# The first block's attention with queries on partitions in the values product, and the softmax division moved to its eviction

## What is computed

```python
o_mla  = rms_norm(mla_attention(h_mla, ...), mla_out_norm[l])       # 6 heads, q.k over 96, v 64 wide
o_diff = diff_attention(h_diff, ..., diff_norm[l], ...)             # 6 heads, two score maps of 32, v 64 wide
o_ch   = rms_norm(chunk_attention(h_ch, chunk_rel_bias[l]), chunk_out_norm[l])   # 4 heads of 64
x = x + jnp.concatenate([o_mla, o_diff, o_ch], axis=-1) @ w_out[l]
x = x + conv_ffn(rms_norm(x, ffn_norm[l]), ...)
```

## Time and profile before

| | us |
|---|---|
| median of 3 runs (lowest, highest) | 3262.74 (3247.85, 3288.86) |
| the profiled execution's own time | 3253.76 |
| its span, first to last instruction | 3252.1 |
| PE busy | 3127.5 (96%) |
| POOL busy | 1364.6 (42%) |
| DVE busy | 1323.3 (41%) |
| ACT busy | 839.6 (26%) |
| mean granted TensorE clock | 0.972 |

### The profile page before, as it was taken

How to read it: one execution, slowest core, us unless ns; L and a number is a source line. 1 busy time by engine, 2 the same in 40 slices (tenths; PEclk the granted TensorE clock), 3 DMA queues, 4 the chain that set the end, 5 groups by cost and what they waited for, 6 DMA issues and landing times.

```text
span 3252.1 us, 40121 instructions
## 1 busy us (share of the span) xinstructions
PE 3127.5 (96%) x14094; PEld 2430.5 (75%) x14094; DVE 1323.3 (41%) x2699; ACT 839.6 (26%) x1855; POOL 1364.6 (42%) x924
## 2 busy tenths in 40 slices
PE   7999999999989999989999999999999999999998
PEld 6666788888656788878666678888686667788886
DVE  5574434243664434353741641121437417411113
ACT  2346211121454212121333320011213333210112
POOL 5210555554211555555223445555452234455552
PEclk9989999999989999999999999999999999999999
DMA  7310566665311566655223546666452235466663
GB/s 251 104 52 27 175 194 193 193 209 180 98 40 53 184 194 194 192 183 175 91 86 115 157 154 187 195 201 193 149 175 91 85 117 159 154 189 190 204 193 101
DMA packets 136516, 494.05 MB, mean 152 GB/s; under 512 B 15280, under 2 KB 15536, under 8 KB 136112
## 3 DMA queue, kind: packets, MB, share of 16 engines
q0 software_dynamic: 66240, 241.20, 24.3%
q1 hardware_dynamic: 68544, 245.40, 23.7%
q10 hardware_dynamic: 1584, 5.40, 0.5%
HBM read 489.84 MB, written 2.10 MB: 151 GB/s over the span
## 4 chain that ended last, share of the span: by engine, by line
PE 93%; DVE 3%; ACT 1%; issue 1%; DMA 0%; POOL 0%; SPq 0%; DVEq 0%; POOLq 0%; ACTq 0%
PE ps L482 25%; PE ps L483 24%; PE ps L484 24%; PE ps L635 6%; PE ps L658 5%; PE ps L648 2%; PE ps L591 1%; PE ps L593 1%; PE ps L592 1%; PE ps L831 1%; PE ps L545 1%; PE ps L859 0%; PE ps L850 0%; DMA w_raw<-weights 0%; DVE lo L962 0%
## 5 line engine op out<-in xcount | busy, mean ns | idle before, releaser
L482 PE MATMUL ps<-hi,w_hi 128*128 128x512 f32 x3216 | 1286.9, 400 | 37.5 <-POOL w_lo L455 15.5
L483 PE MATMUL ps<-hi,w_lo 128*128 128x512 f32 x3216 | 1262.5, 393 | 0.0
L484 PE MATMUL ps<-lo,w_hi 128*128 128x512 f32 x3216 | 1261.4, 392 | 0.0
L455 POOL TENSOR_TENSOR w_lo<-w_raw,w_hi 128x1024 fp32r<-128x1024 f32 x460 | 1106.9, 2406 | 94.2 <-DMA w_hi<-weights 84.9
L450 POOL DMA_DIRECT2D w_hi<-weights x460 | 261.4, 568 | 1751.0 <-PE ps L484 1613.5
L482 PEld LDWEIGHTS ps<-hi,w_hi 128*128 128x128 f32 x3216 | 609.3, 189 | 228.8 <-issue 85.9
L484 PEld LDWEIGHTS ps<-lo,w_hi 128*128 128x128 f32 x3216 | 609.3, 189 | 130.4
L483 PEld LDWEIGHTS ps<-hi,w_lo 128*128 128x128 f32 x3216 | 609.9, 190 | 119.8
L1008 DVE CUSTOM_DVE_ANT_0 pr<-ps,kc 128x128 f32<-128x128 f32 (+1 forms) x208 | 88.8, 427 | 375.7 <-PE ps L635 375.7
L1499 ACT ACTIVATE pT<-ps 128x128 f32<-128x128 f32 (+1 forms) x248 | 97.8, 394 | 372.2 <-PE ps L648 371.9
L1647 ACT ACTIVATE ps<-hb,col 128x512 f32<-128x512 f32 x88 | 68.6, 782 | 381.1 <-DVE hb L991 381.1
(11 more groups left out here) (282 smaller groups left out, 3090.1 us busy)
## 6 DMA issues: line engine op xcount, KB each, us to landing
w_raw<-weights SPq DMA_DIRECT2D x460, 512.0 KB, 3.6
w_hi<-weights POOLq DMA_DIRECT2D x460, 512.0 KB, 4.0
x<-xt SPq DMA_DIRECT2D x8, 256.0 KB, 10.5
out<-x SPq DMA_DIRECT2D x8, 256.0 KB, 2.0
kc<-k ACTq DMA_DIRECT2D x1, 1281.0 KB, 5.6
bias<-relb ACTq DMA_DIRECT2D x2, 512.0 KB, 5.4
bias<-relb ACTq DMA_DIRECT2D x1, 1024.0 KB, 4.8
praw<-pt ACTq DMA_DIRECT2D x2, 512.0 KB, 3.6
```

Of the source, the lines that this page charges most:

```text
L455: nc.gpsimd.tensor_tensor(wlo[s][:, :], raw[s][:, :], whi[s][:, :].bitcast(F32), ALU.subtract).then_inc(w_split, 1)
L482: nc.tensor.matmul(out_ap, w[0], xx[0], start=first, stop=False)
L483: nc.tensor.matmul(out_ap, w[1], xx[0], start=False, stop=False)
L484: return nc.tensor.matmul(out_ap, w[0], xx[1], start=False, stop=last)
```

## The change

- The values product swaps its operands: the transposed weights (128 x 128) are stationary, the values (64 columns) are streamed, and the output has 128 queries on the partitions and 64 channels wide. It goes into the bank that its transposes had, a ring of 3.
- `p` is no longer divided for all keys. DVE evicts each task's 64 columns with the division (`tensor_scalar` by 1/sum) and squares and sums them by a second instruction. For diff heads one small factor, lambda times sum 1 over sum 2, is applied to the second map.
- The output norms' factors come from these sums: no squares on ACT, no sum or spread matmuls (L736, L746, L761, and the last L554 and L545 before `w_out`). The rows are scaled on DVE, and 8 tiles are transposed at the end (`turn_chunk`, 4 transposes each) into banks from which ACT and DVE take the high and low half.
- The slopes go into the queries, so the six `slope_times_distance` tables go away.
- The tasks are in the order diff 0 to 7, chunk 0 to 7, diff 8 to 23, MLA, chunk 8 to 15. Of the dense units only `dq0` and `dk0` remain ahead of the values; 12 units are spread over turns 0 to 23, and the MLA queries, keys and values take turns 24 to 36.
- `tables()` is split: distances first, before the input norm; `angles` is in DVE's side of turn 2, `signed_sine` in that of turn 5.

```diff
+ORDER_1 = ["cq0", "ck0", "cc0", "cc1", "cc2", "dq1", "stats", "dk1", "kr", "sp0", "sp1", "dq2", "dk2", "cq1", "ck1",
+           "Q0", "K0", "Q1", "V0", "V1", "Q2", "Q3", "K1", "Q4", "Q5", "K2", "V2", "V3"]
+FULL = ["cq0", "ck0", "cc0", "cc1", "cc2", "dq1", "dk1", "kr", "dq2", "dk2", "cq1", "ck1"]
+ITEM_AT = {24: "Q0", 25: "K0", 26: "Q1", 27: "V0", 28: "V1", 29: "Q2", 30: "Q3", 31: "K1", 32: "Q4", 33: "Q5", 34: "K2",
+           35: "V2", 36: "V3"}
+TILES_1 = 4 + len(ORDER_1) + 8 + 2 * FF1_C + 8 * len(FF1_GROUPS)
...
-        m_at = cm_at + 3 * KB2
-        alibi = {}
-        for b in range(2):
-            two = [place(f"alibi{b}_{i}", [P, 1280], F32, m_at + i * 5120) for i in range(2)]
-            last_one = place(f"alibi{b}_last", [P, 1280], F32, buf_at[b] + 8 * KB2)
-            alibi[b] = [two[h % 2] for h in range(DIFF_H - 1)] + [last_one]
...
+        quot = lambda s: small[:, s % 16:s % 16 + 1]
+        ss = small[:, 176:240]
+        fac = small[:, 240:272]
...
+            return d[0:8] + c_[0:8] + d[8:24] + m_ + c_[8:16]
...
-        FULL_END = [2 * j + 1 for j in range(8)]
-        AT_STATS, AT_SPREAD, AT_Q, AT_K, AT_V, AT_READY = 16, 19, 23, 29, 32, 38
-
-        AT_DIFF, AT_CH, AT_OUT, AT_OUT2, AT_MLA = 41, 45, 48, 50, (52, 59)
+        QUARTERS = {it: 2 for it in range(24)}
+        QUARTERS.update({12: 0, 13: 4, 14: 4, 15: 0})
+        FULL_END = [1, 3, 5, 7, 9, 11, 13, 14, 17, 19, 21, 23]
+        AT_STATS, AT_SPREAD, AT_KR = 12, 15, 20
+        AT_FACTOR, AT_SCALE = 60, 62
...
+            def attention_1(ts, slots, fill):
+                n = len(ts)
+                on0 = q.on
+                for it in range(-1, n + 3):
+                    if it + 1 < n:
+                        t = ts[it + 1]
+                        if t.more.get("rope"):
+                            pe.wait_ge(rope_done, t.more["rope"])
+                        if t.more.get("kcopy"):
+                            pe.wait_ge(kcopy, t.more["kcopy"])
+                        for tile_n in t.more.get("after", ()):
+                            pe.wait_ge(d_free[BANK[tile_n]], USE[tile_n] + 1)
+                        for lq, rk in t.maps:
+                            if q.s >= 3:
+                                pe.wait_ge(s_free, q.s - 2)
+                            nc.tensor.matmul(ps[:, S_BANK[q.s % 3], 0:t.n], lq, rk, start=True, stop=True).then_inc(s_done, 1)
+                            q.s += 1
+                    if it >= 0:
+                        fill(it)
+                    if 0 <= it - 2 < n:
+                        i, t = it - 2, ts[it - 2]
+                        if t.kind == "diff":
+                            pe.wait_ge(p_ready, t.p0 + 1)
+                        else:
+                            pe.wait_ge(exp_done, t.s0 + 1)
+                        if i >= 3:
+                            pe.wait_ge(on_ready, on0 + i - 2)
+                        for kb in range(t.n // P):
+                            last = nc.tensor.transpose(ps[:, TO_BANK[i % 3], kb * P:(kb + 1) * P],
+                                                       slots(i)[0][t.s0 % 6][:, kb * P:(kb + 1) * P], ident)
+                        last.then_inc(t_done, 1)
+                        q.task += 1
+                    if 0 <= it - 3 < n:
+                        i, t = it - 3, ts[it - 3]
+                        pe.wait_ge(pt_ready, t.id + 1)
+                        if t.more.get("value"):
+                            pe.wait_ge(d_free[BANK[t.more["value"]]], USE[t.more["value"]] + 1)
+                        for kb, v in enumerate(t.vs):
+                            last = nc.tensor.matmul(ps[:, TO_BANK[i % 3], 0:64], slots(i)[1][t.id % 2][:, kb * P:(kb + 1) * P], v,
+                                                    start=(kb == 0), stop=(kb == len(t.vs) - 1))
+                        last.then_inc(pv_done, 1)
+                q.on += n
+
+            def turn_chunk(src, c):
+                if c < len(C_BANK):
+                    pe.wait_ge(on_ready, q.on)
+                else:
+                    pe.wait_ge(lo_ready, q.chunk + c - 3)
+                q.chunks += 1
+                pe.wait_ge(on_scaled, q.chunks)
+                for tb in range(NTB):
+                    last = nc.tensor.transpose(ps[:, C_BANK[c % 4], tb * P:(tb + 1) * P], src[:, tb, :], ident)
+                last.then_inc(chunk_turned, 1)
+
             def attention(ts, slots, fill):
                 n = len(ts)
                 for it in range(-1, n + 3):
...
-                input_norm()
-                dense(1, A, NC_)
-                input_spread()
-                dense(3, A, NC_)
-                values(4, 2, 384, A, need, natural)
+                q.sq += NC_
+                first_sums()
+                values(4, 2, 384, A, need, natural, first_spread)
                 values(2, 4, 256, A, need, natural)
...
-                attention(TASKS["1", l], slots_1(l), fill)
-                pe.wait_ge(r_ready, q.bca)
-                q.sq += 3
-                pe.wait_ge(sq_used, q.sq)
-                sums()
...
+                attention_1(TASKS["1", l], slots_1(l), fill)
+                dn, mn, cn = natural_out(l)
+                for c, src in enumerate(dn + mn):
+                    turn_chunk(src, c)
+
+                def turn_last():
+                    q.chunk -= NC_
+                    for c in range(2):
+                        turn_chunk(cn[c], 6 + c)
+                    q.chunk += NC_
+
                 need = q.chunk
...
-                dense(8, A, NC_, need, (5, mla_factors))
+                dense(8, A, NC_, need, (4, turn_last))
...
+            def attention_1(ts, slots, lam, side):
+                n = len(ts)
+                on0 = q.on
+                for it in range(n + 5):
+                    if it < n:
+                        t, pb = ts[it], slots(it)[0]
+                        for m in range(len(t.maps)):
+                            s = q.s
+                            dve.wait_ge(s_done, s + 1)
+                            if s - 6 in SLOT_TASK:
+                                dve.wait_ge(t_done, SLOT_TASK[s - 6] + 1)
+                            V.tensor_tensor_reduce(out=pb[s % 6][:, 0:t.n], in0=ps[:, S_BANK[s % 3], 0:t.n], in1=t.more["add"],
+                                                   scale=-t.scale, scalar=3.0e38, op0=ALU.add, op1=ALU.min,
+                                                   accum_out=ngm(s)).then_inc(s_free, 1)
+                            q.s += 1
+                    if 1 <= it <= n:
+                        t, pb = ts[it - 1], slots(it - 1)[0]
+                        s = t.s0
+                        dve.wait_ge(exp_done, s + len(t.maps))
+                        if t.kind == "diff":
+                            p0 = pb[s % 6][:, 0:t.n]
+                            link(V.reciprocal(quot(s + 1), rsum(s + 1)))
+                            link(V.scalar_tensor_tensor(out=quot(s), in0=quot(s + 1), scalar=lam, in1=rsum(s), op0=ALU.mult,
+                                                        op1=ALU.mult))
+                            V.scalar_tensor_tensor(out=p0, in0=pb[(s + 1) % 6][:, 0:t.n], scalar=quot(s), in1=p0,
+                                                   op0=ALU.mult, op1=ALU.add).then_inc(p_ready, 1)
+                        V.reciprocal(rinv(on0 + it - 1), rsum(s)).then_inc(rinv_ready, 1)
+                    if 0 <= it - 4 < n:
+                        i, t = it - 4, ts[it - 4]
+                        dve.wait_ge(pv_done, t.id + 1)
+                        dve.wait_ge(rinv_ready, on0 + i + 1)
+                        V.tensor_scalar(t.more["out"], ps[:, TO_BANK[i % 3], 0:64], rinv(on0 + i), None,
+                                        ALU.mult).then_inc(on_ready, 1)
+                    if 0 <= it - 5 < n:
+                        t = ts[it - 5]
+                        dve.wait_ge(on_ready, on0 + it - 4)
+                        if on0 + it - 5:
+                            dve.wait_ge(ss_ready, on0 + it - 5)
+                        V.tensor_tensor_reduce(out=junk[:, :], in0=t.more["out"], in1=t.more["out"], scale=1.0, scalar=0.0,
+                                               op0=ALU.mult, op1=ALU.add, accum_out=t.more["ss"]).then_inc(ss_ready, 1)
+                    side(it)
+                q.on += n
...
+                    elif l == 0 and it == 2:
+                        angles()
+                    elif l == 0 and it == 5:
+                        signed_sine()
...
+                    elif it == AT_FACTOR:
+                        dve.wait_ge(ss_ready, q.on + 56)
+                        link(V.reduce_sum(ss[:, 24:28], ss[:, 24:48].rearrange("p (q h) -> p q h", q=NTB), axis=AX.X))
+                        V.tensor_scalar(fac[:, 0:24], ss[:, 0:24], 1.0 / 64, EPS, ALU.mult, ALU.add)
+                        V.tensor_scalar(fac[:, 24:28], ss[:, 24:28], 1.0 / 384, EPS, ALU.mult, ALU.add).then_inc(var_ready, 1)
+                    elif it == AT_FACTOR + 1:
```

(25 more changed lines are left out.)

518 lines of the change are left out of this document (280 added, 238 removed).

## The result

The changed kernel takes 3235.8 us (median), the kernel before 3255.3 in the same sessions: ratio 0.9937, 95% interval 0.9924 to 0.9949. It is 0.6% faster, within the 2% of "no change"; forecast were 3223 us, with a range of 3172 to 3262. One of the 20 runs of the changed kernel took 3630.2 us at a granted clock of 0.79 for 0.97 and is left out of the ratio. The profiled execution of the changed kernel took 3240.4 us, 4.6 above its median, and its span is 13.4 us shorter than that of before (31 were forecast).

A forecast was written before the change was run, and what follows sets the result against it. PE bounds the kernel (busy 96% of the span, 93% of the chain). Per layer -22 + 1 + 9 + 3.5 - 11 + 4 = -15.5; two layers -31 from the profiled 3253.8 give 3223 us, range 3172 to 3262.

The forecast's parts named there:

- the pitch of 0.11: Values product: each record still takes 0.11 us with 128 stationary and 64 streamed columns, so no gain.
- Turns 16 to 23: Eight filled diff turns (39 us) and the shared key's rope (4.5): 43.5 us for 34.4, +9 a layer.
- three signs of failure: Last window's clock falls, DVE stops PE at most ropes, or new DVE instructions cost over 0.4 us.
- The last window: Turn 40 to the last values product: sums, spreads and their low clock go; 45 us for 56.3, -11 a layer.
- Moved units: Four dense units leave the stretch ahead of the values, -22 us a layer, and return in turns 0 to 23.
- Tables: Layer 0: the 9 us lost to rope tables ahead of attention return as a stall at `angles` in turn 2: 0.
- Turns 24 to 39: DVE decides: it gets 14 us more, has 12 free, not all usable; 54 us for 50.5, +3.5 a layer.
- Shape changes: Between transposes and values product 0.09 us goes, 2 us a layer; the 0.14 before the next scores stays.
- The clock: Rival, 0.06: new values records keep turns 24 to 66 at the lower clock, +61 us a layer, 3345 us.
- The end: Between attention and `w_out`: last eviction, 24 transposes, high-half copy, low half and two scaled chunk tiles: +4 us a layer.
- DVE and POOL: DVE's wait beside POOL's subtraction just moves to the second map's addition and the new squaring: no gain or loss.
- 3155 for a gain from the stream: Extension of the more-gain rival (3188 us, chance 0.24): if the stream also sets the values record, 3155 us.

The follow-up runs named there:

- the wide stream: Changed kernel with each record of the first block's values product streaming 128 value columns (wide) in place of 64 (thin): 3219.0 us, ratio 0.9884.
- The run with full rows: Changed kernel with the chunk heads' scores multiplied over all 128 rows in place of the head's own 64: 3224.8 us, ratio 0.9900.
- the kernel with the four changes: Changed kernel with 128 value columns streamed, squares on ACT, angles before the attention, and DVE's ropes and low halves cut over two turns: 3196.3 us, ratio 0.9809.

## Why the prediction was right, and where it was not

The time is in the range and the class is as forecast, but the size is short: of 31 us came 13 in the profiled execution and 20 by the medians, and part of the agreement is luck. By the forecast's own signs, the pitch of 0.11, the transposes' 0.44 and the stall in turn 2 came. Turns 16 to 23 did not (49.7 us at a clock of 0.84 for about 43 near 1.0), nor did DVE above 90% (82%), and two of the three signs of failure showed: the last window's clock fell, and the new squaring took 0.44 us in the mean of turns 24 to 39. DVE stopped PE at three of seven ropes, not at most. The last window has two errors that cancel: up to the last values product it took 43.7 and 45 us, as forecast (45), while the shape changes gave more than counted and the clock took it. Of the steps:

- *Moved units, right.* Ahead of the attention -23.5 in layer 1 (-22 forecast), and turns -1 to 15 +1.8 (+1).
- *Tables, right within 3 us.* PE stood 4.29 us in turn 2. Against layer 1, layer 0 gained 6.4 us ahead of the attention (9 forecast) and lost 9.0 in turns -1 to 15 (9 forecast).
- *Turns 16 to 23, mis-sized: +9 forecast, +15.4 measured.* The stall of the rope was counted (4.5). Two others in DVE's order were not: 0.77 in turn 16, behind the spread, and 1.27 in turn 19, behind three low halves. The 12 dense records behind each stop take 4.4 to 5.3 us in place of 2.9. Cutting the pieces brought 7.2 and 5.6 us back, so it was their place.
- *Turns 24 to 39, mis-sized: +3.5 forecast, +9 measured.* "Here DVE decides" held: with three quarters of the ropes left out, 10 and 11 us went; with the same ropes spread over two turns, none. I took 14 us more of DVE; it got 48.4 for 38.3 busy, 10 more. What failed is that DVE would fill its free time: it is at 82% of 59.3 us, not above 90%. I had left the clock out here. With the wide stream the window is 55.2 us in both layers, 4.7 over before, near the +3.5; so 4 to 5 of the 9 us came with the thin stream.
- *Shape changes, mis-sized.* I took 0.09 a turn as gained and kept the 0.14 in front of the scores. Measured were 0.32 a turn in MLA turns: 0.09 ahead of the values product, 0.18 behind it and 0.05 behind the scores. The Trainium skill (TensorEngine Tiling, Key Properties) says that a change of the mode drains TensorE. The trace agrees in that such a change costs time and one from 128 to 96 rows does not; the drain itself no row shows. Its sum, 3 us a layer more, would have been nearer. The run with full rows shows that 64 rows against 128 cost much like 64 columns against 128.
- *The clock, a rival at 0.06 that was half right.* I let it decide at a clock of 0.7 in the last window. It fell to 0.87 and 0.85 and cost about what the shape changes gave. My picture, a low clock all through the thin turns, was wrong: fed, they ran at 1.00 for 34.1 us, and it is behind stops that the thin stream stays low. That the swap alone "saves no PE time" came true for another reason than mine: two sizes were off and cancelled (swapped back: 3235.3 against 3235.8). With 128 columns streamed and nothing else changed, 17 us came back.
- *The pitch of 0.11, right.* At 128 stationary columns the stream does not set it, since 2, 64 and 128 streamed columns come alike. That the load does is my argument; no record here has 64 columns both stationary and streamed, so a fixed price of a record is not ruled out. (The 3155 for a gain from the stream should be 3152, 3188 less 2 x 18.)
- *The end, right by its size* (+4 forecast): from the last values product to `w_out` 7.1 us for 3.0 in layer 0, about 6.7 for 4.2 in layer 1. More than half of it ran at a clock of 0.50. Reordered, with the copies ahead of the square root and its table load, the chunks of the kernel with the four changes take 3.38 us for 6.23.
- *DVE and POOL.* The new squaring waited for POOL as L1025 did: one took 2.49 us for 0.22, six of the 64 in layer 0 took 1.2 us or more, all beside a subtraction, and the 16 of turns 24 to 39 took 0.44 in the mean. The Trainium skill (SBUF — State Buffer, Who interferes with whom) has this for two SBUF inputs; the trace agrees for the squaring. The addition of the second map, which I had named too, keeps its 0.75 us, but none of its 48 instructions ran beside one of POOL, so it tells nothing of that. Moving the squares to ACT brought 21 us, but how much of it is load and how much this wait was not tried apart.

```profile
148.35 2.49 DVE L1102 CUSTOM_DVE_ANT_0 junk<-dq 128x64 f32<-128x64 f32 x1
...
298.34 0.22 DVE L1102 CUSTOM_DVE_ANT_0 junk<-vc 128x64 f32<-128x64 f32 x1
```

Open: a window with the thin stream differs from one profiled execution to the next. Layer 1 has the same instructions in the changed kernel and in the run with early angles, yet its turns 24 to 39 took 60.3 us at a clock of 0.76 in one and 57.2 at 0.85 in the other. So single windows carry less than the times do. Behind the same stop of 2.2 us for ACT's copy, the clock fell in five layers of eight with the thin stream, and in neither of two with the wide one. Why it falls and stays low more with the thin stream was not tried.

## What to carry to other kernels

Read the granted clock of each stretch beside its busy time: a record that only gets thinner may come no faster and still cost time. Here, widening the stream of the values records to 128 columns cost nothing in an MLA head and 0.2 us in a chunk head, and gave 17 us. The clock fell behind stops of PE, so look at it behind each of them. Where an engine that works in order feeds the one that sets the pace, what counts is the longest piece of work between two of its deliveries while it has slack, and its load once it has little. Cut the first, and move the second to where its deadline is late. Price a change of the stationary shape at both of its ends, from a row of each kind of neighbour.

## What the hardware showed that I had not expected

- Values records with 64 streamed columns and with 128 come every 0.11 us, at 128x128 stationary. From turn 40 to `w_out`, the seven experiments that stream 128 columns were granted a clock of 0.95 to 1.00, the changed kernel and the five experiments that stream 64 were granted 0.75 to 0.95. The kernel before, with 128 columns and the 24 records of sums, had 0.94 and 0.93.
- Scores with 64 rows of a stationary 128 columns cost 0.14 us more than with 96 or 128 rows before the transposes behind them (0.42 for 0.28), and the values product ahead of them 0.09 more; 96 and 128 rows behave alike.
- A square-and-sum of 64 columns takes DVE 0.22 us and 0.08 to read the sum, and up to 2.49 us beside POOL's subtraction. It takes ACT 0.25 us and 0.19.
